# Seven products in 32 instead of 30 of the 44 k-pair steps of a down projection, in runs of seven and nine, with two pairs' activation sums parked in DRAM

## The reference, cut to what matters

```
D_MODEL = 2048
SEQ = 256
D_FF = 5632
def conv_ffn(h, w_up, conv_w, conv_b, w_down):
    ...
    a, b = jnp.split(u, 2, axis=-1)
    return (jax.nn.silu(a) * b) @ w_down
...
h = rms_norm(x, ffn_norm[l])
x = x + conv_ffn(h, w_ffn_up[l], ffn_conv_w[l], ffn_conv_b[l], w_ffn_down[l])
```

## Time and profile before

| what | us |
|---|---|
| median of 3 runs (lowest, highest) | 1084.19 (1083.81, 1084.48) |
| the profiled execution | 1084.03 |
| its span, first to last instruction | 1082.3 |
| PE busy | 1076.9 |
| DVE busy | 908.5 |
| ACT busy | 629.7 |
| POOL busy | 72.6 |

### The profile page before, as it was taken

How to read it: one execution, slowest core, us unless ns; L and a number is a source line. 1 busy time by engine, 2 the same in 40 slices (tenths; PEclk the granted TensorE clock), 3 DMA queues, 4 the chain that set the end, 5 groups by cost and what they waited for, 6 DMA issues and landing times.

```text
span 1082.3 us, 18185 instructions
## 1 busy us (share of the span) xinstructions
PE 1076.9 (99%) x6549; PEld 930.6 (86%) x6549; DVE 908.5 (84%) x1371; ACT 629.7 (58%) x925; POOL 72.6 (7%) x101
## 2 busy tenths in 40 slices
PE   9999999999999999999999999999999999999998
PEld 8888888888888888888888888888888888888887
DVE  6877988889656678888888888887877899999997
ACT  6677666757554655545555555545555566656663
POOL 4500000000000000000000000000010000000000
PEclk9999999999999999999999999999999999999999
DMA  7644687787788979788887878788897877769882
GB/s 261 195 140 154 193 203 228 195 244 201 227 226 263 262 216 248 218 239 216 251 224 231 243 208 256 224 230 228 250 244 226 238 233 287 281 225 303 287 314 95
DMA packets 184910, 249.08 MB, mean 230 GB/s; under 512 B 9125, under 2 KB 142918, under 8 KB 184598
## 3 DMA queue, kind: packets, MB, share of 16 engines
q1 hardware_dynamic: 170118, 212.30, 60.8%
q0 software_dynamic: 12592, 31.85, 15.6%
q10 hardware_dynamic: 2144, 4.21, 1.2%
HBM read 243.75 MB, written 36.04 MB: 259 GB/s over the span
## 4 chain that ended last, share of the span: by engine, by line
PE 98%; DMA 1%; DVE 1%; ACT 0%; issue 0%; SPq 0%; DVEq 0%; ACTq 0%
PE bank L1728 38%; PE bank L1736 20%; PE bank L2111 6%; PE bank L2113 6%; PE bank L2112 6%; PE bank L1964 3%; PE bank L1796 3%; PE bank L1965 3%; PE bank L1797 3%; PE bank L1798 3%; PE bank L1966 3%; PE bank L1698 1%; DMA slot<-u_sums 1%; PE bank L1703 1%; PE bank L2003 0%; PE bank L1883 0%
## 5 line engine op out<-in xcount | busy, mean ns | idle before, releaser
L727 ACT CAST w_hi<-raw 128x1024 fp32r<-128x1024 f32 x299 | 312.5, 1049 | 255.2 <-PE bank L1736 122.6
L1120 DVE TENSOR_TENSOR w_lo<-raw,w_hi 128x1024 fp32r<-128x1024 f32 x299 | 363.7, 1221 | 108.3 <-ACT w_hi L727 107.7
L1728 PE MATMUL bank<-hs,w_hi 128*128 128x512 f32 x1792 | 423.0, 391 | 0.0
L1728 PEld LDWEIGHTS bank<-hs,w_hi 128*128 128x128 f32 x1792 | 331.2, 188 | 66.4 <-issue 0.9
L1736 PEld LDWEIGHTS bank<-hs,w_lo 128*128 128x128 f32 x1792 | 224.6, 191 | 5.7 <-issue 0.2
L1736 PE MATMUL bank<-hs,w_lo 128*128 128x256 f32 x1792 | 227.3, 283 | 0.0
L1090 ACT CAST hi_slot<-slot 128x1024 fp32r<-128x1024 f32 (+1 forms) x96 | 111.0, 1186 | 69.4 <-DVE slot L1655 36.6
L1639 DVE TENSOR_TENSOR slot_lo<-slot,hi_slot 128x1024 fp32r<-128x1024 f32 (+1 forms) x96 | 128.8, 1387 | 2.8 <-ACT hi_slot L1090 1.9
L2113 PE MATMUL bank<-hi_slot,gated 128*128 128x512 f32 (+1 forms) x202 | 78.2, 387 | 0.0
L2111 PE MATMUL bank<-hi_slot,gated 128*128 128x512 f32 (+1 forms) x202 | 78.2, 387 | 0.0
L1557 DVE SCALAR_TENSOR_TENSOR C<-U,cols,C 128x256 f32<-128x256 f32 x176 | 73.3, 478 | 0.0
(11 more groups left out here) (250 smaller groups left out, 1198.6 us busy)
## 6 DMA issues: line engine op xcount, KB each, us to landing
raw<-in_w_ffn_up_dram SPq DMA_DIRECT2D x176, 512.0 KB, 4.9
u_sums<-in_w_ffn_down_dram POOLq DMA_DIRECT2D x60, 512.0 KB, 7.0
raw<-in_w_in_dram SPq DMA_DIRECT2D x52, 512.0 KB, 4.6
slot<-in_w_ffn_down_dram SPq DMA_DIRECT2D x36, 512.0 KB, 5.4
raw<-in_w_in_dram SPq DMA_DIRECT2D x64, 256.0 KB, 3.3
raw<-in_w_out_dram SPq DMA_DIRECT2D x32, 512.0 KB, 5.3
slot<-u_sums SPq DMA_DIRECT2D x60, 256.0 KB, 6.7
slot<-in_w_ffn_down_dram SPq DMA_DIRECT2D x30, 256.0 KB, 4.9
```

The lines of the kernel that those rows point to most:

```text
L727: act.copy(w_hi[:, i, :], raw[:, i, :]).then_inc(units_hi, 1)
L1120: dve.tensor_tensor(w_lo[:, i, :], raw[:, i, :], w_hi[:, i, :].bitcast(F32), ALU.subtract)\
L1728: m = pe.matmul(banks[b][:, :], w_hi[:, i, c], hs[:, 4 * i + k, :], start=(first and k == 0), stop=(final and k == 3))
```

## The change

The patterns become 32 S and 12 plain steps, with S in runs of 7, 9, 2, 7 and 7. Plain steps now come in three kinds. "C" has its high parts in blocks 0 to 1 and 5 to 6 of the high-part buffer and its raw data in the small slot; "D" has its high parts in blocks 3 to 4 and 5 to 6 and its raw data in the small slot; "c" lies in a large slot, in blocks 0 to 1 and 5 to 6. The wait for a place is worked out per block (`last_piece_in`), no longer per piece of the last user of the slot. Two pairs' activation sums are parked, from the ACT queue, in the up projection; they come back together at steps 5 and 29. The transfers of `x2` are moved to other steps. `add_last(0)` stands behind piece a of step 23 instead of ahead of it. POOL's steps come every 4 pieces instead of 13/3, for 16 instead of 15 pairs.

```
-PATTERNS = ["CCCCSSSSSCSSSSSCSSSSSC", "CCSSCSSSSSCSSSSSCSSSCC"]
+PATTERNS = ["CCCCSSSSSSSDSSSSSSSSSc", "CcSSDSSSSSSSDSSSSSSSDc"]
+KINDS = "".join(PATTERNS)
...
-PARKED_SUM = SEVENS - 1
-PARKED_TURN = 6
-SEVEN_ORDER = [*range(PARKED_TURN), PARKED_SUM, *range(PARKED_TURN, PARKED_SUM)]
+RESIDENT_SUMS = 14
+PARKED_SUMS = SEVENS - RESIDENT_SUMS
+LAST_PARKED_TURN = 6
+FIRST_PARKED_TURN = LAST_PARKED_TURN - PARKED_SUMS + 1
+SEVEN_ORDER = [*range(FIRST_PARKED_TURN), *range(RESIDENT_SUMS, SEVENS), *range(FIRST_PARKED_TURN, RESIDENT_SUMS)]
...
+ADDED_BEHIND = (23, "a")
...
-        if kind == "C" and SMALL_SLOT not in slot_of[-2:]:
+        if kind in "CD":
...
-SUM_STEP = (13, 3)
+SUM_STEP = (4, 1)
...
+        def last_piece_in(q, piece, same_place, blocks):
+
+            last = []
+            for n in range(*blocks(q, piece).indices(7)):
+                users = [piece_number(m, p) for m in range(OLD_RING, q) if same_place(m) for p in pieces_of(m)
+                         if n in range(*blocks(m, p).indices(7))]
+                if users:
+                    last.append(users[-1])
+            return max(last) if last else None
+
+        def raw_piece_before(q, piece):
+            return last_piece_in(q, piece, lambda m: SLOT_OF[m] == SLOT_OF[q], raw_blocks_of)
+
+        def hi_piece_before(q, piece):
+            return last_piece_in(q, piece, lambda m: m % HI_SLOTS == q % HI_SLOTS, blocks_of)
...
-            return {"a": slice(0, 2), "b": slice(2, 4)}[piece]
+            if KINDS[q] in "Dd":
+                return {"a": slice(3, 5), "b": slice(5, 7)}[piece]
+            return {"a": slice(0, 2), "b": slice(5, 7)}[piece]
...
-        FETCH_SUM_AT = 5
-        FETCH_AT = [9, 11, 14, 16]
+        X2_PARTS = [(1, 1), (1, 0), (0, 0), (0, 1)]
+        X2_PARTS_APART = 2 - (PARKED_SUMS - 1)
+        SUMS_BACK_AT = [5, 7]
+        X2_BACK_AT = [[5, 14, 14, 14], [7, 15, 15, 15]]
...
-                if n == PARKED_SUM:
-                    pool.wait_ge(s_split, SEVENS)
-                    pool.dma_start(sum_in_dram_v, at_the_end.bitcast(F32)).then_inc(sum_parked, 16)
...
+            def park_sums(g):
+                act.wait_ge(s_split, g + 1)
+                act.dma_start(sums_in_dram_v[:, g - RESIDENT_SUMS, :, :], at_the_end.bitcast(F32))\
+                    .then_inc(sum_parked, 16)
...
                     split(q, piece)
+                    if (q, piece) == ADDED_BEHIND:
+                        add_last(0)
...
-                    if pair == 1 and at == 0:
-                        add_last(0)
```

More of the change, by code:

```diff
@@ L269, in hybrid_layer @@
         s_tiles += [(sb_at(place, f"s_hi{n}", [P, 3, P], F32R), sb_at(place, f"s_lo{n}", [P, 3, P], F32R))
-                    for n in range(3, SEVENS - 2)]
+                    for n in range(3, RESIDENT_SUMS - 1)]
         s_tiles.append((sb("s_hi_top", [P, 3, P], F32R), sb("s_lo_top", [P, 3, P], F32R)))
         at_the_end = gated[:, KT_FF - 2:KT_FF, 0:3 * P]
[L273 to L276, removed]
+        s_tiles += [[at_the_end[:, n, :].rearrange("p (c m) -> p c m", m=P) for n in range(2)]] * PARKED_SUMS
+        parked_sums = sb_at(list(small), "parked_sums", [P, PARKED_SUMS, 2, 3, P], F32R)
+        sums_in_dram = nc.dram_tensor("s_parked", (P, PARKED_SUMS * 2 * 3 * P), F32)
+        sums_in_dram_v = sums_in_dram.ap().rearrange("p (s n m) -> p s n m", n=2, m=3 * P)
         x2 = sb_at(list(small), "x2", [P, TT, 2 * GT])
@@ L354, in hybrid_layer @@
             sem("summed_step"), sem("s_made"), sem("s_rounded"), sem("s_split"))
-        sum_parked, sum_back = sem("sum_parked"), sem("sum_back")
+        sum_parked, sums_back = sem("sum_parked"), sem("sums_back")
         x2_parked, x2_back = sem("x2_parked"), sem("x2_back")
         down_loaded = {piece: [sem(f"down_loaded_{piece}{n}") for n in range(SLOTS)] for piece in "ab"}
+        four_loaded = {piece: [sem(f"four_loaded_{piece}{n}") for n in range(SMALL_SLOT)] for piece in "ab"}
         t2_made, t4_made = sem("t2_made"), sem("t4_made")
@@ L457, in hi_slot, with in_large_slot, loaded_of, down_loads @@
             return hi_slots[q % HI_SLOTS][:, blocks_of(q, piece), :]
-        def down_loads(q, piece):
+        def in_large_slot(q):
+            return KINDS[q] in "cd"
+        def loaded_of(q, piece):
+            return (four_loaded if in_large_slot(q) else down_loaded)[piece][SLOT_OF[q]]
+        def down_loads(q):
             n = sum(is_seven(*divmod(m, QUADRUPLES)) + 1 for m in range(OLD_RING, q + 1)
-                    if SLOT_OF[m] == SLOT_OF[q])
+                    if SLOT_OF[m] == SLOT_OF[q] and in_large_slot(m) == in_large_slot(q))
             return 16 * n
         def wait_for_down(engine, q, piece):
-            engine.wait_ge(down_loaded[piece][SLOT_OF[q]], down_loads(q, piece))
+            engine.wait_ge(loaded_of(q, piece), down_loads(q))
         def wait_until_used(engine, number):
@@ L566, in _, with fetch_sums @@
                 load_channels(g * 2 + Q_UP + 1, w_up_v, g * GC + D_FF)
+            def fetch_sums(pair):
+                if pair == 0:
+                    sp.wait_ge(gated_lo, UP_GROUPS)
+                    sp.wait_ge(sum_parked, 16 * PARKED_SUMS)
+                else:
+                    sp.wait_ge(stored, 16)
+                sp.dma_start(parked_sums[:, :, :, :, :].rearrange("p s n c m -> p (s n c m)").bitcast(F32),
+                             sums_in_dram.ap()).then_inc(sums_back, 16)
             def fetch_x2(pair, part):
@@ L584, in wait_for_slot @@
             def wait_for_slot(q, piece):
-                before = slot_before(q)
+                before = raw_piece_before(q, piece)
                 if before is not None:
-                    wait_until_used(sp, piece_before(q, piece, before))
+                    wait_until_used(sp, before)
                 elif SLOT_OF[q] == 2:
@@ L626, in _ @@
                         load_four(pair, at)
[L627 to L636, removed]
+                    if at == SUMS_BACK_AT[pair]:
+                        fetch_sums(pair)
+                    for part in range(len(X2_PARTS)):
+                        if at == X2_BACK_AT[pair][part]:
+                            fetch_x2(pair, part)
         @block.gpsimd
@@ L2168, in seven @@
                 first, final = turn == 0, turn == SEVENS - 1
-                if n == PARKED_SUM:
-                    pe.wait_ge(sum_back, 16 * (pair + 1))
-                    s_hi, s_lo = parked_sum[:, 0, :, :], parked_sum[:, 1, :, :]
+                if n >= RESIDENT_SUMS:
+                    pe.wait_ge(sums_back, 16 * (pair + 1))
+                    s_hi, s_lo = [parked_sums[:, n - RESIDENT_SUMS, r, :, :] for r in range(2)]
                 else:
```

42 lines of the change are left out of this document (23 added, 19 removed).

## The result

The changed kernel takes **1085.86 us** in the median of 22 runs (1085.29 to 1086.56), the kernel before 1084.23 in 22 runs on the same chip (1083.81 to 1085.1). The ratio is **1.0015, with a 95% interval of 1.0009 to 1.0021**: 1.6 us slower, less than the 0.2% within which the prediction spoke of no change, and forecast as 1085.7. The profiled execution has a span of 1084.3 us.

A forecast was written before the change was run, and what follows sets the result against it. DVE was taken to bound the down projection's runs of S: 875.07 + 188.1 + 0.54 + 0.5 puts step 41's b at 1064.2, PE at 1066.1 against 1064.54, so +1.5 us: 1085.7, range 1083.4 to 1088.3.

The forecast's parts named there:

- The 6 matmuls: Down projection, PE: two plain steps become S, saving 1.36 us; with 0.7 us of old gaps, 2.06 were DVE never late.
- The ledger of DVE: Steps 4 to 41's b: 31 S intervals, 6 plain steps and one merge make 188.1 us of DVE work, 6.2 more.
- the ledger of the kernel before: Same steps before the change: 181.9 us of DVE work, 1057.0 without waits against 1061.16 measured, so 4.2 us of waits.
- The waits: DVE's waits in the down projection: 0.54 us stay at steps 6 and 7, 3.5 go, 0.5 comes at step 24.
- All three of 3.5 us that the prediction let go: DVE's old waits at steps 8, 11 and 25, for transfers and a high-part place, would vanish: 3.5 us in all.
- The new one: Step 24: add_last(0) between step 23's splits delays ACT's high part, so DVE starts 0.5 us late; bounds 0 and 1.1.
- Piece b of step 41: Near the last S: DVE starts it at 1064.2, PE at 1066.1 against 1064.54 before, making the end 1.5 us later.
- Where PE waits: Gaps behind DVE's low part at steps 18 to 20, 32 to 33 and 39 to 41, 3.3 to 3.6 us.
- The up projection: Copies paced 8% denser cost ACT 0.5 us more waiting for weight loads, covered by its reserve: 0, otherwise +0.5.
- The rule against the rows: DVE operations would not overlap, an S costing 5.58 us and DVE's work 195.8, time 1093; chance 0.01.
- DVE does not keep up: Judges the rival that DVE keeps up by an unseen reserve, saving matmuls and old gaps: 1082.1; chance 0.12.
- Waits for transfers behind step 12: Rival: transfer waits return at steps 15 to 18 or 25 to 28, time 1087 to 1089; chance 0.24.

The follow-up runs named there:

- Experiment 7: The change with the first sum of six S made in DRAM and add_last(0) back ahead of step 23: 1082.33 us against 1083.95 before, ratio 0.9985.
- experiment 4: The change with every plain step's high parts back in the lower blocks 0 to 1 and 2 to 3: 1086.16 us against 1083.95 before, ratio 1.0018.
- Experiment 1: The change with 30 S instead of 32, the rest of its code kept: 1083.17 us against 1083.83 before, ratio 0.9991.
- experiment 3: The change with the additions of add_last(0) back ahead of step 23: 1085.12 us against 1083.83 before, ratio 1.0009.
- experiment 5: The change with the plain step 42 near the end moved forward into the second run: 1086.83 us against 1083.83 before, ratio 1.0023.
- experiment 2: Four unread DVE operations added behind step 24: in the change 1088.34 us, in the 30 S kernel with its new layout 1085.04, both against 1083.95 before.
- experiment 6: The change with the first of the two weight sums of every S made on GpSimd instead of DVE: 1095.81 us against 1083.83 before, ratio 1.0105.

## Why the prediction held

*The 6 matmuls*: gone, and with the old gaps worth 2.06 us were DVE never late. Experiment 7 is that case, nearly: its stage is 182.29 - 180.34 = 1.95 us shorter than before.

*The ledger of DVE*: 188.1 us without waits from step 4 to step 41. Measured 189.40, with 0.33 (step 6), 0.40 (step 7) and 0.44 (20.07 less 19.63, step 24) of waits, so 188.2. An S took 5.39 as forecast. The start was 875.09 for 875.07. In the ledger of the kernel before, the wait at step 25 is 1.86 us in the trace (piece b starts at 984.27, step 24's at 977.02) and not 1.7; that is why the waits listed there sum to 4.0 and not to 4.2.

*The waits*: step 6 as forecast; step 7 0.40 for 0.21, since its `u_sums` were 0.17 late beside ACT's 0.17. All three of 3.5 us that the prediction let go are gone, one of them on experiment 4's evidence by the upper blocks. Those of steps 8 and 25 were not brought back alone, so their causes are argued; that they are gone is no chance of one execution, for in the traces of the change and of experiments 1, 3, 4, 5 and 7 both steps take 5.39 or 5.40 us. The new one is 0.44 where 0.5 was taken, and experiment 3 confirms its cause.

*Piece b of step 41*: 1066.30, forecast 1066.1. The span follows, 1084.3 against 1082.3. Of these 2.0 us 1.76 are this piece's; the rest lies behind it. The medians differ by 1.6.

*Where PE waits*: at steps 18 to 20, 32 and 33, 40 and 41, all among those named. The sum is 3.5 us, forecast as 3.3 to 3.6. At step 39, which was named too, it did not wait, with 0.19 us of lead left. The leads themselves came as forecast: 0.90 for 1.1 at step 10, 3.44 for 3.7 at step 12, 1.26 for 1.0 at step 24.

*The up projection*: mis-sized. "8% more" of ACT's 6.0 us for raw weights should have been 6.5, and 18.0 were measured, the longest single wait 4.5 instead of 2.1. ACT's reserve there covers that too; the term stayed 0, by less of a margin than was argued. This part of the forecast came out right with some luck.

*The rule against the rows* (the Trainium skill, VectorE: DVE Perf Modes, section "The DRAIN you can't avoid"): it would have made 1093. In the change an S takes 5.39 from start to start over eight in a row, and its durations sum to 5.58, so the trace disagrees with it here too. The same paragraph goes on to say that a next operation that is not held starts earlier, which the prediction left out. Its count for the kernel before is also off: 29 x 5.58 + 8 x 2.44 + 8.2 is 189.5, not 189.8; the comparison stands.

*The rivals*: DVE does not keep up (experiment 2, gaps of PE). Waits for transfers behind step 12: none in the change. (The loads of an S are five blocks of 256 KB, 1.31 MB, beside 1.05 for a plain step; the prediction's 1.28 and 1.05 are in different units.) Neither of the signs that would have made the forecast wrong is there: DVE's first S starts at 872.51, and PE is never idle in the up projection.

## What to carry to other kernels

A change that saves 1.36 us on the engine with 99% of the span can cost more on the one with 84%, if the stage where it lies is full on both. Before trading work between engines, add up the second engine's time from start to start over that stage, and spend no more than the lead it has; a dose of idle operations measures that lead. Where the reserve is spent, look for work of the full engine that a transfer can do, rather than an engine that blocks it while it works, as GpSimd blocked VectorE here.

## What the runs showed of the hardware

GpSimd's sum of 512 columns took 1833 ns in the mean (experiment 6), and took turns with DVE's operations that read two tensors in SBUF: in 31 of 32 cases it ended 1.14 to 1.20 us behind the end of the DVE operation that it had started beside, and a DVE operation that started beside it took 1.0 to 1.1 us longer. Moving 0.72 us per S off DVE made most of its S 0.37 longer.

Successive independent operations of DVE overlap: a split of 1024 columns lasts 1.22 us and the next starts 1.13 to 1.14 behind it. After a wait for DVE the second matmul of PE comes 0.33 us behind the first instead of 0.227.

Copies from DRAM to DRAM at an 8% denser pace went with more waits of ACT for raw weights: 6.0 us in the one trace of the kernel before, and 15.6 to 37.5 in the traces of the change and of all the experiments, while the median landing of those loads moved from 4.9 to between 4.8 and 5.6. Experiment 1, which has the pace but no more copies than before, has 15.6; the change has 18.0, and experiment 3, whose up projection is the change's, 37.5. So the sum of such waits says little from one execution, and how much of the rise is the pace's is not shown. PE was not idle between 400 and 860 us in any of them.
